# POOL's weight-rest subtraction in pieces of 512 columns, with another layout, first norm and split order, in a two-layer hybrid block

## What is computed

```
for l in range(2):
    sh1, sc1, g1, sh2, sc2, g2 = silu(c) @ mod_w[l] + mod_b[l]
    h  = rmsnorm(x, norm1_w[l]) * (1 + sc1) + sh1          # latent and context, each with its own c
    p  = h @ w_in[l]                                       # split into the three mixers' inputs and gates
    ym, ya, yr = mlstm(p), window_attention(p), retention(p)
    y  = sum(sigmoid(gate_b) * (y_b @ w_br_b)) @ w_out[l]  # b = m, a, r
    x  = x + g1 * y
    h2 = rmsnorm(x, norm2_w[l]) * (1 + sc2) + sh2
    a, b = split(h2 @ ffn_up[l])
    x  = x + g2 * ((silu(dwconv(a) + bias) * b) @ ffn_down[l])
out = rmsnorm(x, final_norm_w)
```

## Time and profile before

| | |
|---|---|
| median of 3 runs | 3207.92 us |
| lowest, highest | 3203.05, 3226.49 us |
| the profiled execution's own time | 3214.93 us |
| its span | 3213.0 us |
| PE busy | 2970.5 us, 92% |
| PEld, DVE, ACT, POOL busy | 2619.0, 1229.5, 959.3, 1115.2 us |
| mean granted clock of TensorE | 0.963 |

### The profile page before, as it was taken

How to read it: one execution, slowest core, us unless ns; L and a number is a source line. 1 busy time by engine, 2 the same in 40 slices (tenths; PEclk the granted TensorE clock), 3 DMA queues, 4 the chain that set the end, 5 groups by cost and what they waited for, 6 DMA issues and landing times. The chain is left out here.

```text
span 3213.0 us, 47607 instructions
## 1 busy us (share of the span) xinstructions
PE 2970.5 (92%) x19520; PEld 2619.0 (82%) x19520; DVE 1229.5 (38%) x2775; ACT 959.3 (30%) x1610; POOL 1115.2 (35%) x608
## 2 busy tenths in 40 slices
PE   5899899999999998999999879989999999799996
PEld 3888877898888997888888658887898789778885
DVE  3555425523332024333333545534523320344445
ACT  3222214432232112222222133323532231232332
POOL 1222320053335333333333233331054345354443
PEclk8999999999999997999999979999999999899998
DMA  5111120022222115111211222121022322322222
GB/s 199 53 66 47 47 73 14 8 83 80 79 80 92 54 53 210 66 66 57 75 54 65 80 70 77 72 92 40 8 96 95 116 79 92 119 80 101 88 99 85
DMA packets 39671, 249.78 MB, mean 78 GB/s; under 512 B 4513, under 2 KB 4897, under 8 KB 14113
## 3 DMA queue, kind: packets, MB, share of 16 engines
q1 hardware_dynamic: 36576, 236.25, 20.8%
q10 hardware_dynamic: 2880, 10.49, 0.8%
HBM read 236.23 MB, written 10.49 MB: 77 GB/s over the span
## 5 line engine op out<-in xcount | busy, mean ns | idle before, releaser
L2018 POOL TENSOR_TENSOR w_rest<-raw,w_head 128x2048 fp32r<-128x2048 f32 (+2 forms) x172 | 740.0, 4303 | 1130.8 <-ACT w_head L1133 1121.7
L759 PE MATMUL psum_products<-w_head,h_head 128*128 128x256 f32 x2368 | 680.1, 287 | 8.1 <-POOL w_rest L2018 8.1
L759 PE MATMUL psum_products<-w_rest,h_head 128*128 128x256 f32 x2368 | 667.1, 282 | 0.0
L759 PE MATMUL psum_products<-w_head,h_rest 128*128 128x256 f32 x2368 | 666.4, 281 | 0.0
L759 PE MATMUL psum_products<-h_head,w_head 128*128 128x512 f32 (+3 forms) x1696 | 603.9, 356 | 15.3 <-POOL h_rest L2054 9.8
L759 PE MATMUL psum_products<-h_head,w_rest 128*128 128x512 f32 (+3 forms) x1696 | 601.0, 354 | 0.0
L759 PE MATMUL psum_products<-h_rest,w_head 128*128 128x512 f32 (+3 forms) x1696 | 600.8, 354 | 0.0
L759 PEld LDWEIGHTS psum_products<-w_head,h_head 128*128 128x128 f32 x2368 | 451.7, 191 | 10.7 <-POOL w_rest L2018 8.6
L1133 ACT ACTIVATE w_head<-raw 128x2048 fp32r<-128x2048 f32 (+2 forms) x172 | 308.2, 1792 | 506.2 <-PE psum_products L759 457.4
L759 PEld LDWEIGHTS psum_products<-w_rest,h_head 128*128 128x128 f32 x2368 | 451.9, 191 | 0.4
L759 PEld LDWEIGHTS psum_products<-w_head,h_rest 128*128 128x128 f32 x2368 | 450.5, 190 | 0.0
(11 more groups left out here) (254 smaller groups left out, 4031.5 us busy)
## 6 DMA issues: line engine op xcount, KB each, us to landing
raw<-in_stream SPq DMA_DIRECT2D x190, 1024.0 KB, 4.7
raw<-in_stream SPq DMA_DIRECT2D x20, 512.0 KB, 3.3
residual<-stage ACTq DMA_DIRECT2D x16, 512.0 KB, 3.3
stage<-residual SPq DMA_DIRECT2D x14, 512.0 KB, 4.7
mods_b<-in_stream SPq DMA_DIRECT2D x5, 1024.0 KB, 22.6
mods_a<-in_stream SPq DMA_DIRECT2D x3, 1024.0 KB, 13.8
x_in<-in_x SPq DMA_DIRECT2D x4, 512.0 KB, 8.6
stage<-in_x SPq DMA_DIRECT2D x4, 512.0 KB, 4.8
```

The source lines that it names most:

```text
L759: return nc.tensor.matmul(o, a, b, start=start, stop=stop)
L2018: G.tensor_tensor(wl[:, s["sp"] % 2, 0:n], place_of(s), wh[:, s["sp"] % 2, 0:n].bitcast(F32), ALU.subtract).then_inc(*ev.mark("pool", "res ...
```

## The change

Five edits:

1. **Split in pieces.** POOL's subtraction (L2018) is issued in pieces of 512 columns: four instructions for a slot of 2048 columns, two for 1024, one for 128. PE, ACT and SP still wait for the last of them.
2. **First norm.** `par` is issued ahead of `const` and `x_in`. Square writes its output into the memory of `h_head` (a place for each tile, not needed yet) and no longer waits for PE; the scaled copy of tile k-1 waits for the turn of tile k-3.
3. **Affine and rest.** `affine_k` of pair j follows the vectors of pair j at once. The subtraction for `h_rest` is a step of its own, `rest_k`, that stands one pair later.
4. **Split ahead of `mvo`.** In the first mLSTM head of each layer the parts marked `open` are the last two and no longer the first two, so the split of the next slot stands before part 0 and not before part 2.
5. **Layout.** The fillers are now 0, 192 and 192 bytes: what began 64 bytes past a multiple of 128 begins on one, and `w_head` and `w_rest` begin 64 bytes past one. The arena is 192 bytes smaller, and the MLP's places start 128 bytes later in it.

```diff
-ARENA_BYTES = 74 * 1024 - 224
+ARENA_BYTES = 74 * 1024 - 416
...
+                step("affine_k", j=j)
                 if j:
-                    step("affine_k", j=j - 1)
-            step("affine_k", j=3)
+                    step("rest_k", j=j - 1)
+            step("rest_k", j=3)
...
-                step("mvo", s, 1, l=l, gen=h, hd=hd, ctx=ctx, pair=p, part=p, open=p < 2)
+                step("mvo", s, 1, l=l, gen=h, hd=hd, ctx=ctx, pair=p, part=p, open=p > 0)
...
-        sb("half_line", [P, 16])
...
-        sb("other_half", [P, 16])
+        sb("filler", [P, 48])
...
-        sb("half_line_too", [P, 16])
+        sb("filler_too", [P, 48])
...
-        R = Region(8 * 1024)
+        R = Region(8 * 1024 + 128)
...
+            sp.dma_start(par[:], ins["params"]).then_inc(*ev.mark("par_in", "par", by=16))
             sp.dma_start(const[:], ins["consts"]).then_inc(*ev.mark("const_in", "const", by=16))
...
-            sp.dma_start(par[:], ins["params"]).then_inc(*ev.mark("par_in", "par", by=16))
...
-                        if k >= 2:
-                            act.wait_ge(*ev.at("x_turn", k - 2))
-                        nc.scalar.activation(xs[:, k % 2], xin[:, k], ACT.Square, accum_out=small[:, cc:cc + 1]).then_inc(
-                            *ev.mark("act", "x_ss", k))
+                        nc.scalar.activation(hh.rearrange("p a b -> p (a b)")[:, k * D:(k + 1) * D], xin[:, k], ACT.Square,
+                                             accum_out=small[:, cc:cc + 1]).then_inc(*ev.mark("act", "x_ss", k))
                     if k >= 1:
...
+                        if k >= 3:
+                            act.wait_ge(*ev.at("x_turn", k - 3))
...
+                elif kind == "rest_k":
                     for k in (2 * st["j"], 2 * st["j"] + 1):
...
-                    G.tensor_tensor(wl[:, s["sp"] % 2, 0:n], place_of(s),
-                                       wh[:, s["sp"] % 2, 0:n].bitcast(F32), ALU.subtract).then_inc(
-                                           *ev.mark("pool", "rest", s["n"]))
+                    for a in range(0, n, SLOT // 4):
+                        b = min(n, a + SLOT // 4)
+                        G.tensor_tensor(wl[:, s["sp"] % 2, a:b], place_of(s)[:, a:b],
+                                        wh[:, s["sp"] % 2, a:b].bitcast(F32), ALU.subtract).then_inc(
+                                            *ev.mark("pool", "rest", s["n"]))
```

## The result

| | before | after |
|---|---|---|
| median of the runs | 3209.06 us (4 runs) | 3167.57 us (4 runs, 3162.41 to 3170.7) |
| ratio to before | | 0.9842, 95% interval 0.9809 to 0.9876 |
| span of the profiled execution | 3213.0 us | 3164.6 us |
| its own time | 3214.93 us | 3166.39 us |
| mean granted clock | 0.963 | 0.965 |

The changed kernel is 1.6% faster by the ratio on record, 1.3% by the two medians; both lie within the interval. 3174 was forecast, with 3148 to 3200 as its range. The total is close; the sum behind it is less so, as the stages will show. Lines of DVE and POOL have new numbers: L1842 is L1843 now, L1845 L1846, L1624 L1625, L1628 L1629, L1805 L1806, L2018 L2021.

A forecast was written before the change was run, and what follows sets the result against it. PE, busy 92% of the span, was taken as the bound. Terms -22.5 - 13.2 + 1.7 - 6.3 - 2.6 - 1.5 + 7.7 = -36.7 us gave 3178.2 or 3171.2, stated as 3174, range 3148 to 3200.

The forecast's parts named there:

- The start: First norm, edits 2 and 3: last h_rest ends at 44.4 in place of 66.9, -22.5 us, bounds 10 to 25.
- The split ahead of mvo: First mLSTM head of each layer, edit 4: both PE gaps and the slow clock behind them go, -13.2 us.
- its result is wanted after 14 more matmuls, so I cost it at nothing: Behind the mvo split: DVE's gate-value chain gets about 1.5 us later, hidden by 14 matmuls, cost 0.
- the 3 us that I had named for the lost cover: Behind the mvo split: the gate chain's delay costs up to 3 us if the matmuls' cover is gone.
- the clock's 5.1 us: Behind the two mvo gaps: PE does half the work at lower clock, up to another 5.1 us comes back.
- The pieces' own cost: Four remaining PE waits for w_rest each grow by 0.42 us because POOL's subtraction is in pieces, +1.7 us.
- The heads: mLSTM heads: DVE gets turns between pieces, three PE gaps shrink by 2.1 us, -6.3, and clock behind them -2.6.
- the port rival: POOL keeps the port, DVE waits for all four pieces; those terms fall away, 3177 us; chance 0.10.
- Attention: Attention: a similar DVE wait behind POOL shortens with the pieces, -1.5 us.
- MLP, layer 1: Seventeen steps: DVE's turns make POOL's subtraction 1.85 us later, 0.45 beyond the slack, +7.7 us, bounds 0 and +20.
- Layout: Edit 5: tensors move by odd numbers of 64 bytes, relation of h to w stays, 0 us.
- the layout moves PE's pace: Rival: PE's pace moves by 1%, 30 us either way, 3144 or 3204; chance 0.10 faster, 0.05 slower.

The follow-up runs named there:

- e4_layout: The kernel before with edit 5 (the layout) alone; 3192.74 us, ratio 0.9929.
- l192: The kernel before with the filler other_half 192 bytes long in place of 64, so w_head less h_head is 192 modulo 256; 3195.1 us beside 3218.07, ratio 0.9943.
- e5_mvo: The kernel before with edit 4 (the split ahead of mvo) alone; 3212.21 us beside 3212.66, ratio 1.0003.

## Why the prediction was right, point by point

**The start** (-22.5). Right in mechanism, a little large: 20.6 in the changed kernel, 19.7 alone. ACT began at 8.47, as estimated. What was too short is the 4.0 us from the last landing to the last factor: PE took the last vectors' matmuls at a granted clock of 0.50, which the estimate left out.

**The split ahead of mvo** (-13.2). The step that failed is "its result is wanted after 14 more matmuls, so I cost it at nothing". The product's two gaps went. The gate chain was not in the way, but L813's wait for POOL's whole step was, 2.9 and 2.4 us, each close to the 3 us that I had named for the lost cover and did not take. And the clock's 5.1 us is not seen in the time: alone, the edit gave 6 to 9 us in the heads, lost 6 in attention 0 in its one profile, and measured no gain (6 us faster to 8 slower).

**The pieces' own cost** (+1.7). Right in kind, somewhat small: the four waits for `w_rest` that stay grew from 3.81, 4.69, 1.08 and 1.10 us to 4.83, 5.10, 1.76 and 1.76, 2.8 us together. A subtraction in four pieces took 5.09 us in the median, 0.48 more than the 4.61 before.

**The heads** (-8.9). DVE got its turn, as the earlier trace rows said; the port rival is out. heads0 gave 12.3 alone: 7.8 us less waiting (6.3 was the term) and 4.8 of clock (2.6 was the term). What was missed is layer 1. There the subtraction meets a chain of three short DVE instructions, and each waits for a piece of its own. Before, then after:

```profile
1944.23 3.30 DVE L1805 SCALAR_TENSOR_TENSOR small<-m_nd 128x2 f32<-128x2 f32 x1
...
1942.90 4.61 POOL L2018 TENSOR_TENSOR w_rest<-raw,w_head 128x2048 fp32r<-128x2048 f32 x1 [9.34 <-ACT w_head L1133]
```

```profile
1889.26 1.23 DVE L1806 SCALAR_TENSOR_TENSOR small<-m_nd 128x2 f32<-128x2 f32 x1
1890.52 1.22 DVE L1817 TENSOR_TENSOR small<-small,gm 128x1 f32<-128x1 f32 x1
1891.67 1.35 DVE L1819 TENSOR_TENSOR small<-small,gm 128x1 f32<-128x1 f32 x1
1893.05 0.17 DVE L1830 RECIPROCAL small<-small 128x2 f32<-128x2 f32 x1
...
1887.93 5.07 POOL L2021 TENSOR_TENSOR w_rest<-raw,w_head 128x512 fp32r<-128x512 f32 x4 [9.32 <-ACT w_head L1133]
```

The three are through 4.9 us after POOL's start before and 5.1 after, so they gain nothing, and POOL is 0.5 us later. In heads1 PE waited 9.4 us for `m_y` with the pieces alone, where it had waited 2.7: that is the +6.6 us of the stage. Why these waits grow is not shown, and the pieces are not all of it: with whole subtractions they came to 6.9 us in e4_layout and 9.1 in l192. In the changed kernel heads1 is 11 to 16 us longer than with whole subtractions, of which 4 to 5 are these waits and 9 to 13 the granted clock.

**Attention** (-1.5). 9 us alone; 7.2 of it is clock, and the 1.8 that are left are close to the term.

**MLP, layer 1** (+7.7). The cost of a step was right, the number of steps was not. I put the subtraction 1.85 us later and PE 0.45; it is 1.57 (6.17 in place of 4.6), and PE waits 0.46 to 0.48. But ten steps have this wait and not seventeen, 4.7 us together; the stage cost +4.4 alone and +6.2 between everything-but-the-pieces and the changed kernel. It was hidden in the total by the layout's -4.3 in the same stage.

**Layout** (0). Wrong. "The relation of `h` to `w` stays, so I take 0": odd against even 64-byte places stays, but the difference went from 64 to 192 modulo 256, and that was the relation to look at. The rival "the layout moves PE's pace" had the sign, at about two thirds of its size, and the pace of unchanged shapes did move by over 1% from start to start (233.2 to 229.1 ns), which the prediction had named as a sign of being wrong; the profile's own means show only 0.7%.

Summed: by their ratios start, layout and pieces are worth about 19, 23 and 8 us and edit 4 nothing; the product of the four ratios is 0.985, the changed kernel's 0.9842. The forecast had 22.5, 0, 1.0 (its five terms on the pieces together) and 13.2. That 36.7 came near the 41.5 us between the medians, or the 48.4 of span, is in good part luck: the missing 23 of the layout and 7 of the pieces went one way, the surplus of edit 4 and of the start, 17 together, the other. Only the start and the turns of DVE in the heads are right in mechanism and near in size.

## What to carry to other kernels

Long POOL instructions set the delay of DVE's SBUF-only instructions; cutting them helped a single DVE instruction, or two, in the way of PE, did nothing for a chain of three in four pieces, and cost POOL each turn. So the piece is to be chosen by stage. Before an instruction is moved earlier in a queue, look for waits on the whole of that queue, not only for waits on its result. Before a stage's difference is put down to an edit, take out what the granted clock took in that stage. A layout change is to be costed by the difference of the operands' addresses, and if no row of a trace shows the new difference, the range has to hold it.

## What the runs showed of the hardware

- fp32r matmuls issued back to back are slower or faster by the address of the moving operand less that of the stationary one, modulo 256 bytes. The range over all kernels and pairs of tensors here, mean ns from start to start:

```
moving less stationary     0                64                128              192
512 columns                227.5            229.0 to 230.1    232.6            233.2
256 columns                119.6 to 119.8   116.3 to 117.8    118.7 to 119.0   113.4 to 116.0
```

  The 512-column figures are h over w, and w over u for 64 (229.0 to 230.1) and 128. At 256 columns they are w over h, h over w and w over y; 128 is w over y alone, in the two kernels with all at equal places. The best difference for one width is the worst for the other.
- 256-column products have two paces, 113 and 118 ns, and two executions of one kernel divide them differently (1,273 and 1,853 of 1,920).
- In the places shown DVE gets one instruction at each boundary of two POOL instructions: with pieces of 1.24 us it waits 1.2 to 1.3 us, and with pieces of 2.35 us it waits 2.36 and 2.33.
- The granted clock can stay at its lower level for 23.7 us while PE shows no gap (e5_mvo, 525.4 to 549.1, in attention's short matmuls), after it fell behind a gap of 1.0 us.
